# The opening of a two-block kernel: one change to the order of its loads and to the shape of two kinds of weight block

## The chip, the cores and the metric

The kernel runs on one core of a Trainium2 chip. The metric is device time in microseconds (us) of one launch. In the profile PE is TensorE (matmuls; PEld is its weight load), DVE is VectorE, ACT is ScalarE, POOL is GpSimd, and SP is SyncE, which here only issues transfers. "SPq" and "ACTq" rows are transfers issued by SP and ACT. Everything is float32.

## The reference

The program computes one Conformer-style block and then two layers of a second block on x (512 tokens x 1024). Only what the opening computes matters here:

```python
sc_l = jax.nn.silu(c)
mod_l = sc_l @ w_mod[0] + b_mod[0]                    # (1024) x (1024 x 6144)
sh1_l, s1_l, g1_l, sh2_l, s2_l, g2_l = jnp.split(mod_l, 6, axis=-1)
hl = rms_norm(xl, norm1_g) * (1 + s1_l) + sh1_l
u = hl @ w_pw1 + b_pw1                                # 1024 x 2048
a, gate = jnp.split(u, 2, axis=-1)
u = a * jax.nn.sigmoid(gate)
u = dwconv(u, w_dw) + b_dw                            # width 31, in 8 segments of 64
u = jax.nn.silu(layer_norm(u, ln_g, ln_b)) @ w_pw2 + b_pw2
xl = xl + g1_l * u
xl = xl + g2_l * (square(relu(modulate(rms_norm(xl, norm2_g), sh2_l, s2_l) @ w1)) @ w2)
```

The second block has its own modulation matrix in each layer (`ada_w_2`, 1024 x 6144 each), an attention and a convolution mixer, and a mixture of 16 experts in each layer.

## The kernel before

**Weights.** All weight matrices are streamed by SP through a ring of six slots of 2 MB (`RING`, `BLK`). The list `stream` is written out once, in order of use; entry n takes the next slot, and SP issues it when the block that held the slot has been released (`owner_release`: a semaphore and the value it must reach). A block is 1024 rows x 512 columns, loaded as 128 partitions x 8 x 512, so that each contiguous piece in memory is 2 KB (`blk`).

**Modulation.** Nine rounds (`mod_gemv`, L914 to L924) each compute 2048 modulation values from four blocks. PE multiplies the stationary silu(c) by the block's rows: 8 steps k of 128 rows, and in each 4 matmuls for the 4 groups q of 512 columns. Before, block q holds all rows of group q, and the round waits for all four blocks before its first matmul. Rounds 1 and 2 lie in the convolution stage, rounds 3 to 8 in the first multilayer perceptron, one after each fourth tile of `mlp_w1`. After a round, ACT copies the row out of PSUM (`mod_row`, L614), PE transposes it (L929), ACT copies that (`mod_turned`, L621), and POOL adds the bias and makes the gains (L473 to L502).

**Vectors.** 33 small transfers bring the vectors (c, gains, biases, convolution taps) as rows into `vec_rows`. Before, ACT issues all of them at its start (L550), and then the six transfers that make up `small_in` (four `lam` vectors and two router matrices, L577 and L579). PE turns the rows into columns in two tiles (`T_V`), DVE copies these to `vecT` (L1367, L1372), and ACT takes silu(c) from there (L632).

**The order of the opening** is the order in which each engine's code is written. SP: x, the constants `K` (1 MB in one transfer), a wait for all 33 vectors, then the ring. PE: the transposes of x (`T_X`), of the vectors (`T_V`), the mean of squares (`norm_stat(NORM1)`, L898), modulation round 0, its transposes, then the pointwise product. ACT: silu(c), the squares (L597), the root (L603), and the copies of round 0. DVE: the copies of x, those of the vectors, the `lam` sums (L1382), and then `scale(NORM1)`: a reciprocal (L1342) and eight products into hT (L1344), of which ACT shifts each (L610).

**The pointwise product** `pw1` (PE, L878) makes 16 output tiles of 128 channels, two for each j (gate, then a). Before, the gate columns of four j are one block and the a columns of the same four j another. Two pairs of blocks serve the 16 tiles. A depthwise convolution on PE (L966) stands behind each second j.

Of the kernel before, what the change touches and what calls it, by code (L numbers as in the profile page):

```python
# [12 lines left out]
P = 128  # L13
D = 1024
DT = D // P
N = 512
# [6 lines left out]
TAPS = 31  # L23
PAD = TAPS // 2
SHIFTS = 4
# [4 lines left out]
HD = 64  # L30
# [34 lines left out]
KW = _at  # L65

# [35 lines left out]
def block_kernel(nc, A, out):  # L102
# [22 lines left out]
    def add_mod(rnd):  # L125
        return [add(blk(mods[rnd // 3], 0, (rnd % 3) * 2048 + q * N), ("mod_row", rnd + 1)) for q in range(4)]
# [97 lines left out]
    for n, (src, slot) in enumerate(stream):  # L224
        if n == FIRST:
            MOE_LOADS[0] = list(loads)
            loads = [x + MOE_BLOCKS // RING for x in loads]
        loads[slot] += 1
        landed_at.append((slot, 16 * loads[slot]))
        prev_of.append(prev[slot])  # L230
        prev[slot] = n
# [8 lines left out]
    with ExitStack() as ctx:  # L240
# [49 lines left out]

        def carve(base, at, *shape):
# [59 lines left out]
        for name in (  # L351
            "vec_in", "x_in", "ctx_in", "const_in", "small_in", "stored",
# [28 lines left out]
        def arrived(eng, n):  # L381
            slot, value = landed_at[n]
            eng.wait_ge(landed[slot], value)
            return slot_ap(stream[n][1])
# [4 lines left out]
        BIASED = {NORM1: 0, LN: 1, NORM2: 2, MIX0: 3, CTXN: 4, FFN0: 5, MIX1: 6, FFN1: 7}  # L389

# [3 lines left out]
        def _(sp):  # L394
            def load(n):
# [5 lines left out]
                sp.dma_start(slot_ap(slot), src).then_inc(landed[slot], 16)  # L401
# [50 lines left out]
        def _(pool):  # L452
# [57 lines left out]
            pool.wait_ge(S["const_in"], 16)  # L510
# [31 lines left out]
        def _(act):  # L542

            g0 = [("c", 0), ("c_2", 8), ("norm2_g", 32), ("norm1_g", 24), ("conv_b_pw1", 48), ("conv_b_dw", 64),
                  ("conv_ln_g", 72), ("conv_ln_b", 80), ("conv_b_pw2", 88)]
            n_vec = 0

            def rows(dst, src):
                nonlocal n_vec
                act.dma_start(dst, src).then_inc(S["vec_in"], 16)  # L550
                n_vec += 1

            for name, at in g0:
                w = A[name].shape[1] // P
                rows(vec_rows[at:at + w, 0, :], A[name][0].rearrange("(r p) -> r p", p=P))
            for name, at in (("c_ctx_2", 16), ("final_g", 40)):
                rows(vec_rows[at:at + 8, 0, :], A[name].rearrange("(r p) -> r p", p=P))
            for name, at in (("norm_mix_2", 96), ("norm_ffn_2", 112)):
                rows(vec_rows[at:at + 16, 0, :], A[name].rearrange("l (r p) -> (l r) p", p=P))
            rows(vec_rows[0:48, 1, :], A["b_mod"][0].rearrange("(r p) -> r p", p=P))  # L560
            rows(vec_rows[48:96, 1, :], A["ada_b_2"][0].rearrange("(r p) -> r p", p=P))
            rows(vec_rows[96:120, 1, :], A["conv_w_2"][0].rearrange("k (r p) -> (k r) p", p=P))
            for m, name in enumerate(("attn_q_norm_2", "attn_k_norm_2")):
                for half in range(2):
                    rows(vec_rows[120 + m:121 + m, 1, half * HD:(half + 1) * HD], A[name])
            rows(vec_rows[122:123, 1, :], A["attn_subln_2"])
            rows(vec_rows[0:48, 2, :], A["ada_b_2"][1].rearrange("(r p) -> r p", p=P))
            for g in range(ROUNDS):
                n = min(SHIFTS, TAPS - SHIFTS * g)
                rows(vec_rows[32 * (g % 4):32 * (g % 4) + 32, 3 + g // 4, 0:32 * n].rearrange("q (k i) -> q k i", k=n),  # L570
                     A["conv_w_dw"][0][SHIFTS * g:SHIFTS * g + n].rearrange("k (q i) -> q k i", i=32))
            for m, j in enumerate(DVE_CONV):
                dst = vec_rows[0:TAPS, 5, :] if m == 2 else vec_rows[48 + TAPS * m:48 + TAPS * (m + 1), 2, :]
                rows(dst, A["conv_w_dw"][0][:, j * P:(j + 1) * P])
            assert n_vec == N_VEC
            for m, name in enumerate(("lam_q1_2", "lam_k1_2", "lam_q2_2", "lam_k2_2")):
                act.dma_start(lam_in[:, m, :], A[name][0].partition_broadcast(P)).then_inc(S["small_in"], 16)  # L577
            for layer in range(2):
                act.dma_start(rw[:, layer, :, :], A["router_w_2"][layer].rearrange("(k p) e -> p k e", p=P))\  # L579
                    .then_inc(S["small_in"], 16)  # L580

# [282 lines left out]
        def _(pe):  # L864
# [49 lines left out]
            def mod_gemv(rnd):  # L914
                ws = [arrived(pe, n) for n in B_MOD[rnd]]
# [773 lines left out]
```

## Time and profile before

| | us |
|---|---|
| median of 3 runs | 2659.02 (2658.41 to 2660.11) |
| the profiled execution's own time | 2660.16 |
| its span, first to last instruction | 2658.4 |
| PE busy, matmuls | 2385.5 (90%) |
| DVE, ACT, POOL busy | 707.2, 414.4, 60.9 |
| mean transfer rate | 213 GB/s, 565.49 MB |

The page cuts the span into 40 slices of 66 us. PE is busy for 4 tenths of the first slice and for 9 or 10 in most others; the transfers are busy for 8 tenths of it. A row of a timeline gives start and duration in us, the engine, the line and the operation, and how many instructions were merged; in brackets stands the idle time ahead of it and what ended it. A matmul of float32 appears as two records. What counts in such a kernel is what PE waits for, and where; idle time on the other engines costs nothing by itself.

### The profile page before, as it was taken

Reading aid. Unit: us, or ns where it says so; the run is one execution under the profiler, and the core shown is the slowest. Engines: PE = TensorE matmul, PEld = TensorE weight load, DVE = VectorE, ACT = ScalarE, POOL = GpSimd, SP = SyncE. Lnnn points to the kernel's source line nnn. Section 1 sums busy time; section 2 is a strip of 40 time slices with the busy share of each in tenths; the row PEclk is TensorE's granted clock in tenths of the full one; section 3 lists DMA queues with packets and bytes.
Section 4 is the critical chain, followed back from the end, with each engine's and each line's share of the span. In section 5 each row is a group of like instructions: output and inputs, shape, how many; then the busy total and the mean of one; then the engine's idle time right before and its main releaser. Section 6 shows DMA issues by size and latency. Waiting matters only on the chain.

```text
span 2658.4 us, 21610 instructions
## 1 busy us (share of the span) xinstructions
PE 2385.5 (90%) x8882; PEld 1080.2 (41%) x8882; DVE 707.2 (27%) x958; ACT 414.4 (16%) x683; POOL 60.9 (2%) x66
## 2 busy tenths in 40 slices
PE   4999899999999999677699899998999699989997
PEld 1443344444444455443334344442444334434443
DVE  2683200000006632772411111113111411111112
ACT  1223200000004111551300000001000201000000
POOL 1000000000010000000100000000000100000000
PEclk7999999999999999887899999999999899999999
DMA  8307276138300002000488999888110488999985
GB/s 293 124 35 284 96 275 230 63 133 293 143 0 32 32 32 95 0 1 0 190 354 378 391 391 380 379 379 337 42 64 0 190 346 374 388 390 390 385 379 221
DMA packets 110548, 565.49 MB, mean 213 GB/s; under 512 B 8344, under 2 KB 8734, under 8 KB 85918
## 3 DMA queue, kind: packets, MB, share of 16 engines
q1 hardware_dynamic: 105856, 563.09, 52.6%
q10 hardware_dynamic: 4638, 1.64, 0.3%
q8 instruction: 39, 0.64, 0.1%
q14 instruction: 15, 0.12, 0.0%
HBM read 562.61 MB, written 2.10 MB: 212 GB/s over the span
## 4 chain that ended last, share of the span: by engine, by line
PE 79%; DMA 9%; DVE 6%; issue 3%; ACT 2%; SPq 1%; ACTq 0%; DVEq 0%
PE psum L878 38%; PE psum L1242 19%; DMA ring<-in_moe_w_down_dram 9%; PE psum L1292 5%; PE psum L1256 5%; PE psum L1080 2%; PE psum L922 2%; PE psum L966 1%; PE psum L1149 1%; PE psum L898 1%; PE psum L1128 1%; DVE rstd L1536 1%; DVE rstd L1342 1%; PE psum L1193 1%; PE psum L1142 1%
## 5 line engine op out<-in xcount | busy, mean ns | idle before, releaser
L878 PE MATMUL psum<-hT,ring 128*128 128x512 f32 x1632 | 718.0, 600 | 23.7 <-ACT hT L610 18.4
L1242 PE MATMUL psum<-ring,arena 128*64 128x512 f32 x3072 | 681.7, 600 | 57.5 <-DMA ring<-in_moe_w_down_dram 23.7
L878 PEld LDWEIGHTS psum<-hT,ring 128*128 128x128 f32 x1632 | 312.5, 193 | 419.7 <-issue 412.9
L1242 PEld LDWEIGHTS psum<-ring,arena 128*64 128x64 f32 x3072 | 245.8, 138 | 460.6 <-issue 460.6
L878 PE MATMUL psum<-arena,ring 128*128 128x512 f32 x640 | 275.2, 592 | 0.0
L878 PEld LDWEIGHTS psum<-arena,ring 128*128 128x128 f32 x640 | 121.6, 190 | 153.1 <-issue 153.1
L1611 DVE TENSOR_TENSOR arena<-psum,arena 128x512 f32<-128x512 f32 x32 | 33.7, 1054 | 445.7 <-PE psum L1242 445.7
L1256 PE MATMUL psum<-arena 128*128 128x128 f32 x1024 | 121.9, 281 | 23.4 <-DVE arena L1602 23.4
L1256 PEld LDWEIGHTS psum<-arena 128*128 128x128 f32 x1024 | 119.0, 197 | 35.1 <-DVE hT L1622 32.1
L1292 PE MATMUL psum<-arena 128*128 128x512 f32 x256 | 123.3, 618 | 0.0
L1354 DVE SCALAR_TENSOR_TENSOR xT<-psum,modv,xT 128x512 f32<-128x512 f32 x32 | 24.0, 750 | 308.5 <-PE psum L878 308.5
L1622 DVE TENSOR_TENSOR hT<-hT,psum 128x512 f32<-128x512 f32 x128 | 88.0, 688 | 34.1 <-PE psum L1292 34.1
L1447 DVE TENSOR_TENSOR arena<-arena 128x512 f32<-128x512 f32 x32 | 22.1, 692 | 244.2 <-ACT arena L705 244.2
L922 PE MATMUL psum<-ring,cpad 128*32 128x512 f32 x576 | 66.3, 614 | 17.2 <-DMA ring<-in_w_mod_dram 17.2
L1619 DVE COPY arena<-psum 128x512 f32<-128x512 f32 x16 | 11.1, 692 | 262.7 <-PE psum L1242 262.7
L597 ACT ACTIVATE sq<-xT 128x512 f32<-128x512 f32 x56 | 35.1, 629 | 260.4 <-DVE xT L1354 228.9
L1292 PEld LDWEIGHTS psum<-arena 128*128 128x128 f32 x256 | 39.4, 188 | 83.6 <-DVE hT L1622 63.0
L1421 DVE SCALAR_TENSOR_TENSOR arena<-arena,vecT 128x512 f32<-128x512 f32 x90 | 72.3, 803 | 3.2
L1142 PE MATMUL psum<-K,arena 128*128 128x128 f32 x144 | 29.7, 355 | 48.4 <-DVE arena L1530 33.3
L705 ACT ACTIVATE arena<-psum 128x512 f32<-128x512 f32 x32 | 19.1, 597 | 311.8 <-PE psum L878 311.8
L1465 DVE RECIPROCAL rstd<-rms 128x512 f32<-128x512 f32 (+1 forms) x18 | 50.8, 2819 | 44.1 <-ACT rms L744 44.0
L898 PE MATMUL psum<-sq,K 128*128 128x512 f32 (+1 forms) x80 | 41.4, 665 | 13.1 <-ACT sq L597 12.8
(182 smaller groups left out, 1445.1 us busy)
## 6 DMA issues: line engine op xcount, KB each, us to landing
ring<-in_moe_w_gate_dram SPq DMA_DIRECT2D x64, 2048.0 KB, 16.8
ring<-in_moe_w_up_dram SPq DMA_DIRECT2D x64, 2048.0 KB, 14.2
ring<-in_moe_w_down_dram SPq DMA_DIRECT2D x64, 2048.0 KB, 14.5
ring<-in_ada_w_dram SPq DMA_DIRECT2D x24, 2048.0 KB, 10.8
ring<-in_mlp_w_dram SPq DMA_DIRECT2D x16, 2048.0 KB, 12.8
ring<-in_w_mod_dram SPq DMA_DIRECT2D x12, 2048.0 KB, 13.1
ring<-in_conv_w_pw_dram SPq DMA_DIRECT2D x6, 2048.0 KB, 18.6
ring<-in_conv_w_in_dram SPq DMA_DIRECT2D x6, 2048.0 KB, 19.0
```

What stands on the lines that cost most here:

```text
L597: act.activation(sq[:, g % 2, 0:width], src[:, j, :], ACT.Square).then_inc(S["sq_ready"], 1)
L878: ins = pe.matmul(bank[:, 0:width], w[:, k, col:col + P], src(k), start=start and k == 0, stop=stop and k == kts - 1)
L898: ins = pe.matmul(psum[:, STAT, 0:width], const("ones_d"), sq[:, g % 2, 0:width], start=j == 0, stop=j == DT - 1)
L922: ins = pe.matmul(psum[32 * q:32 * q + 32, MISC, :], cpad[:, k, :], ws[q][:, k, :], start=k == 0, stop=k == DT - 1, skip_group_check=True)
L1080: ins = pe.matmul(psum[:, t % 6, 0:width], src, w[:, k, 0:width], start=k == 0, stop=k == DT - 1)
L1142: ins = pe.transpose(psum[:, 6 + k // 4, (k % 4) * P:(k % 4 + 1) * P], attn[:, it % 2, k * P:(k + 1) * P], ident)
L1242: ins = pe.matmul(psum[64 * e:64 * e + 64, bank + nh, :], src[:, 4 * h + k, 64 * e:64 * e + 64], w[:, k, nh * N:(nh + 1) * N], start=h == ...
L1256: ins = pe.matmul(psum[:, 6 + fj // 4, (fj % 4) * P:(fj % 4 + 1) * P], h_tok[:, tt, fj * P:(fj + 1) * P], sel[:, tt, :, :].rearrange("p a ...
L1292: pe.matmul(psum[:, 6 + fj % 2, :], y_sb[:, fj * P:(fj + 1) * P], gselT, start=True, stop=True)\
L1421: ins = dve.scalar_tensor_tensor(out=acc, in0=u, scalar=w, in1=acc, op0=ALU.mult, op1=ALU.add)
L1465: link(dve.reciprocal(rstd[:, 0:w], rms[:, 0:w]))
L1622: dve.tensor_tensor(hT[:, fj, :], hT[:, fj, :], psum[:, 6 + fj % 2, :], ALU.add)\
```

## The change

SP no longer waits for the vectors. It issues x and the first 512 columns of `K` (the identity and the three averaging matrices), 15 of the 33 vector transfers (convolution taps, modulation biases, `conv_w_2`), the four blocks of modulation round 0, the first pointwise block, then the rest of `K` (1504 columns, with its own semaphore `const_rest`, for which POOL waits before it builds the taps), and goes on with the ring. ACT issues the other 18 vector transfers; the six transfers of `small_in` now come behind silu(c).

A modulation block is now 256 whole rows of the round's 2048 columns (128 x 2 x 2048, contiguous pieces of 8 KB), in all nine rounds, and PE waits for block k/2 only when step k comes to it. A pointwise block now holds the gate and the a columns of two j, 256 columns each (two transfers of 1 MB, contiguous pieces of 1 KB, one semaphore), so that four blocks serve the 16 tiles; each is released when its four tiles are done.

PE computes `norm_stat(NORM1)` ahead of the vectors' transposes, ACT does squares and root ahead of silu(c), and DVE does the reciprocal ahead of its wait for the gains, and the `lam` sums behind `scale(NORM1)`. In the other norms the wait for the gains stands behind the reciprocal too.

```diff
     def add_mod(rnd):
-        return [add(blk(mods[rnd // 3], 0, (rnd % 3) * 2048 + q * N), ("mod_row", rnd + 1)) for q in range(4)]
+        a, part = divmod(rnd, 3)
+        return [add(mods[a][256 * b:256 * b + 256, 2048 * part:2048 * part + 2048].rearrange("(k p) n -> p k n", p=P),
+                    ("mod_row", rnd + 1)) for b in range(4)]
...
-    def add_pw1(b):
-        last = T_PW1[4 * b + 3] + 2
-        B_PW1[b] = (add(blk(A["conv_w_pw1"][0], 0, D + b * N), ("tile_done", last - 1)),
-                    add(blk(A["conv_w_pw1"][0], 0, b * N), ("tile_done", last)))
-
-    add_pw1(0)
-    add_pw1(1)
+    pw1_rows = A["conv_w_pw1"][0].rearrange("(k p) n -> p k n", p=P)
+    for b in range(4):
+        B_PW1[b] = add([pw1_rows[:, :, 256 * b + D * (1 - m):256 * b + D * (1 - m) + 256] for m in range(2)],
+                       ("tile_done", T_PW1[2 * b + 1] + 2))
...
-            sp.dma_start(K[:, :], A["const_k"]).then_inc(S["const_in"], 16)
-
-            sp.wait_ge(S["vec_in"], 16 * N_VEC)
+            sp.dma_start(K[:, 0:K_FIRST], A["const_k"][:, 0:K_FIRST]).then_inc(S["const_in"], 16)
+            load_rows(sp, "late")
             for n in range(FIRST):
                 load(n)
+                if n == 4:
+                    sp.dma_start(K[:, K_FIRST:KW], A["const_k"][:, K_FIRST:KW]).then_inc(S["const_rest"], 16)
...
+            load_rows(act, "early")
...
+            act.wait_ge(S["pads_zero"], 4)
+            squares(NORM1, xT, emptied(T_X))
+            root(NORM1)
             act.wait_ge(FREE["dve"], T_V + 2)
-            act.wait_ge(S["pads_zero"], 4)
             act.activation(cpad[:, :, 0:3], vecT[:, 0:24].rearrange("p (i k) -> p k i", i=3), ACT.Silu)\
                 .then_inc(S["c_silu"], 1)
-            squares(NORM1, xT, emptied(T_X))
-            root(NORM1)
...
             def mod_gemv(rnd):
-                ws = [arrived(pe, n) for n in B_MOD[rnd]]
...
                 for k in range(DT):
+                    if k % 2 == 0:
+                        w = arrived(pe, B_MOD[rnd][k // 2])
                     for q in range(4):
-                        ins = pe.matmul(psum[32 * q:32 * q + 32, MISC, :], cpad[:, k, :], ws[q][:, k, :],
+                        ins = pe.matmul(psum[32 * q:32 * q + 32, MISC, :], cpad[:, k, :], w[:, k % 2, q * N:(q + 1) * N],
...
+            norm_stat(NORM1)
             pe.wait_ge(S["vec_in"], 16 * N_VEC)
...
-            norm_stat(NORM1)
             mod_gemv(0)
...
                 dve.wait_ge(S["rms_ready"], n + 1)
                 link(dve.reciprocal(rstd[:, 0:width], rms[:, 0:width]))
+                if made:
+                    dve.wait_ge(S["gains"], made)
...
+            scale(NORM1, xT, hT, gain[:, 0, :], made=1)
             dve.wait_ge(S["small_in"], 16 * 6)
```

SP's instructions at the start, before. `hT` receives x, `arena` the vector rows; each row is the line, the operation, the operands, the shape, what it waits for, and a count.

```order
L429 DMA hT<-in_x_dram 128x4x1024
L430 DMA K<-in_const_k_dram 128x2016
L401 DMA ring<-in_w_mod_dram 128x8x512 [waits vec_in]
L401 DMA ring<-in_w_mod_dram 128x8x512 x3
L401 DMA ring<-in_conv_w_pw_dram 128x8x512 x2
L401 DMA ring<-in_conv_w_pw_dram 128x8x512 [waits mod_row] x2
L401 DMA ring<-in_w_mod_dram 128x8x512 [waits mod_row] x2
```

The same place now:

```order
L471 DMA hT<-in_x_dram 128x4x1024
L472 DMA K<-in_const_k_dram 128x512
L400 DMA arena<-in_conv_w_dw_dram 32x4x32 x7
L400 DMA arena<-in_conv_w_dw_dram 32x3x32
L400 DMA arena<-in_conv_w_dw_dram 31x128 x3
L400 DMA arena<-in_b_mod_dram 48x128
L400 DMA arena<-in_ada_b_dram 48x128
L400 DMA arena<-in_conv_w_dram 24x128
L400 DMA arena<-in_ada_b_dram 48x128
L443 DMA ring<-in_w_mod_dram 128x2x2048 x4
L441 DMA ring<-in_conv_w_pw_dram 128x8x256 x2
L477 DMA K<-in_const_k_dram 128x1504
```

The wait for `vec_in` is gone from SP, and 15 small transfers stand where it was.

PE's instructions between the transposes of x and the pointwise product, before (`arena` holds the vector rows, `sq` the squares, `cpad` silu(c)):

```order
L888 MATMUL psum<-K,arena 128x128 [waits dve_free,vec_in]
L888 MATMUL psum<-K,arena 128x123
L898 MATMUL psum<-sq,K 128x512 [waits sq_ready] x8
L922 MATMUL psum<-ring,cpad 32x512 [waits landed3,landed2,c_silu,landed1,landed0]
L922 MATMUL psum<-ring,cpad 32x512 x31
L929 MATMUL psum<-K,mod_rows 128x128 [waits mod_row_sb]
L878 MATMUL psum<-hT,ring 128x512 [waits h_ready,landed4,dve_free]
```

The same place now:

```order
L909 MATMUL psum<-sq,K 128x512 [waits sq_ready] x8
L899 MATMUL psum<-K,arena 128x128 [waits dve_free,vec_in]
L899 MATMUL psum<-K,arena 128x123
L934 MATMUL psum<-ring,cpad 32x512 [waits landed0,c_silu]
L934 MATMUL psum<-ring,cpad 32x512 x7
L934 MATMUL psum<-ring,cpad 32x512 [waits landed1]
L934 MATMUL psum<-ring,cpad 32x512 x7
L934 MATMUL psum<-ring,cpad 32x512 [waits landed2]
L934 MATMUL psum<-ring,cpad 32x512 x7
L934 MATMUL psum<-ring,cpad 32x512 [waits landed3]
L889 MATMUL psum<-hT,ring 128x512 [waits h_ready,dve_free,landed4]
```

The statistics moved ahead of the vectors, and the one wait for four blocks became four waits of one block each.

## Rows read from the trace of the kernel before

**Rows 1.** Chain of waits, 0 to 450 us: start, us, what.

```profile
59.10 3.36 DVE rstd L1342
...
64.25 30.19 PE psum L878 x64
...
208.89 6.87 PE psum L922 x64
...
340.33 7.00 PE psum L922 x64
...
375.44 7.00 PE psum L922 x64
```

**Rows 2.** Timeline of PE, 0 to 70 us.

```profile
11.63 5.17 PE L888 MATMUL psum<-K,hT 128*128 128x128 f32 x32 [11.63 <-DMA K<-in_const_k_dram]
16.75 0.93 PE L888 MATMUL psum<-K,arena 128*128 128x128 f32 x6
20.38 9.21 PE L898 MATMUL psum<-sq,K 128*128 128x512 f32 x16 [2.70 <-ACT sq L597]
46.79 9.73 PE L922 MATMUL psum<-ring,cpad 128*32 128x512 f32 x64 [17.20 <-DMA ring<-in_w_mod_dram]
57.24 0.65 PE L929 MATMUL psum<-K,mod_rows 128*128 128x128 f32 x4 [0.71 <-ACT mod_rows L614]
```

**Rows 3.** What SP's transfers waited for, to 460 us: total, times, longest.

```profile
SPq L401 <- DMA arena<-in_conv_w_dw_dram: 15.0, 1, 15.0
```

**Rows 4.** Timeline of SP, 0 to 460 us.

```profile
1.25 0.49 SPq L430 DMA_DIRECT2D K<-in_const_k_dram  x1
16.72 15.24 SPq L401 DMA_DIRECT2D ring<-in_w_mod_dram  x4
```

**Rows 5.** Ring blocks issued at 16.72; 26.12; 215.8 and 216.2 us: issue to landing.

```profile
DMA to landing us min/median/max: 13.5/13.5/13.5
...
DMA to landing us min/median/max: 20.4/20.4/20.4
...
DMA to landing us min/median/max: 7.8/10.3/12.8
```

**Rows 6.** Transfers by issue, 0 to 60 us: count, KB each, us to landing.

```profile
hT<-in_x_dram SPq DMA_DIRECT2D x1, 2048.0 KB, 8.1
...
K<-in_const_k_dram SPq DMA_DIRECT2D x1, 1008.0 KB, 10.3
rw<-in_router_w_dram ACTq DMA_DIRECT2D x2, 64.0 KB, 11.4
```

**Rows 7.** Windows: PE, PEld, DVE, ACT, POOL busy; granted clock, DMA share, GB/s.

```profile
29.60:46.80 17.20, 0.01 (x2) 0.04 (x3) 0.46 (x4) 0.80 (x2) 0.00 (x0) 0.56 1.05 387
64.25:69.40 5.15, 5.15 (x7) 2.15 (x8) 3.97 (x8) 5.13 (x8) 0.00 (x0) 0.51 1.05 387
1630.00:1700.00 70.00, 62.51 (x303) 27.38 (x301) 10.97 (x15) 6.04 (x8) 0.00 (x0) 1.00 0.93 393
```

**Rows 8.** Timeline of ACT, 0 to 70 us.

```profile
9.16 5.06 ACTq L550 DMA_DIRECT2D arena<-in_conv_w_dw_dram  x11
...
16.09 1.10 ACTq L579 DMA_DIRECT2D rw<-in_router_w_dram  x2
...
19.58 0.23 ACT L632 ACTIVATE cpad<-vecT 128x24 f32<-128x24 f32 x1 [0.95 <-DVE vecT L1372]
...
56.59 0.60 ACT L614 ACTIVATE mod_rows<-psum 128x512 f32<-128x512 f32 x1 [26.18 <-PE psum L922]
```

**Rows 9.** Timeline of DVE, 0 to 70 us.

```profile
12.79 0.69 DVE L1363 COPY xT<-psum 128x512 f32<-128x512 f32 x1 [11.89 <-PE psum L888]
...
18.09 1.23 DVE L1367 COPY vecT<-psum 128x128 f32<-128x128 f32 x4
...
62.49 5.44 DVE L1344 SCALAR_TENSOR_TENSOR hT<-xT,gain,rstd 128x512 f32<-128x512 f32 x8
```

**Rows 10.** What PE's instructions waited for, 64.3 to 500 us: total, times, longest.

```profile
PE psum L878 <- ACT hT L610: 12.4, 2, 6.4
```

More of the change, by code:

```diff
@@ L227, in block_kernel @@
             loads = [x + MOE_BLOCKS // RING for x in loads]
-        loads[slot] += 1
+        loads[slot] += len(src) if isinstance(src, list) else 1
         landed_at.append((slot, 16 * loads[slot]))
@@ L289, in slot_ap, with slot_like @@
             return ring[:, slot * BLK:(slot + 1) * BLK].rearrange("p (k n) -> p k n", k=DT)
+        def slot_like(slot, src):
+            whole = ring[:, slot * BLK:(slot + 1) * BLK]
+            if isinstance(src, list):
+                return [carve(whole, m * BLK // 2, src[m].shape[1], src[m].shape[2]) for m in range(2)]
+            return whole.rearrange("p (k n) -> p k n", k=src.shape[1])
         def carve(base, at, *shape):
@@ L400, in load @@
                     sp.wait_ge(S[name], value)
-                sp.dma_start(slot_ap(slot), src).then_inc(landed[slot], 16)
+                if isinstance(src, list):
+                    for m, dst in enumerate(slot_like(slot, src)):
+                        sp.dma_start(dst, src[m]).then_inc(landed[slot], 16)
+                else:
+                    sp.dma_start(slot_like(slot, src), src).then_inc(landed[slot], 16)
             def load_experts(layer):
@@ L556, in _ @@
[L556 to L580, printed above, removed]
+            load_rows(act, "early")
@@ L628, in _ @@
             act.sem_inc(S["y_act"], 1)
+            act.wait_ge(S["pads_zero"], 4)
+            squares(NORM1, xT, emptied(T_X))
+            root(NORM1)
             act.wait_ge(FREE["dve"], T_V + 2)
[L631 removed]
             act.activation(cpad[:, :, 0:3], vecT[:, 0:24].rearrange("p (i k) -> p k i", i=3), ACT.Silu)\
                 .then_inc(S["c_silu"], 1)
[L634 to L635 removed]
+            for m, name in enumerate(("lam_q1_2", "lam_k1_2", "lam_q2_2", "lam_k2_2")):
+                act.dma_start(lam_in[:, m, :], A[name][0].partition_broadcast(P)).then_inc(S["small_in"], 16)
+            for layer in range(2):
+                act.dma_start(rw[:, layer, :, :], A["router_w_2"][layer].rearrange("(k p) e -> p k e", p=P))\
+                    .then_inc(S["small_in"], 16)
             mod_row(0)
@@ L1335, in link, with scale @@
                 dve.wait_ge(S["dve_link"], link_n[0])
-            def scale(n, src, dst, gains, width=N):
+            def scale(n, src, dst, gains, width=N, made=0):
                 if n:
@@ L1385, in _ @@
                 dve.wait_ge(S["lam_sum"], m + 1)
-            dve.wait_ge(S["gains"], 1)
-            scale(NORM1, xT, hT, gain[:, 0, :])
             def glu(j):
@@ L1440, in _ @@
                 dve.tensor_tensor(xT[:, j, :], xT[:, j, :], tmp[:, j % 2, :], ALU.add).then_inc(S["x_pw2"], 1)
-            dve.wait_ge(S["gains"], 3)
-            scale(NORM2, xT, hT, gain[:, 1, :])
+            scale(NORM2, xT, hT, gain[:, 1, :], made=3)
             for half in range(2):
@@ L1451, in _ @@
             scale(FINAL, xT, xT, vec("final_g"))
-            dve.wait_ge(S["gains"], 8)
-            scale(MIX0, xT, hT, gain[:, 2, :])
+            scale(MIX0, xT, hT, gain[:, 2, :], made=8)
             scale(CTXN, xcT, hcT, gain[:, 3, :], NC)
```

51 lines of the change are left out of this document (35 added, 16 removed).

## The prediction

> **What bounds the kernel now.** I read the page first: PE is busy for nine tenths of most slices and for four tenths of the first, while the transfers are busy there. The whole question is therefore when the first pointwise matmul starts. The chain of waits has it at 64.25 us, as the head of an unbroken run on PE [rows 1]. In the timeline of PE before that [rows 2] the reader is to see five short pieces and one idle stretch that dwarfs the rest: 17.20 us ahead of modulation round 0, ended by a transfer of `w_mod`. SP's waits say why it came late: SP stood 15.0 us for the vectors [rows 3] and issued the first modulation block at 16.72 [rows 4]. That block landed 13.5 us later, at 30.2, and the fourth, issued at 26.12, landed 20.4 later, at 46.5 [rows 5], where PE starts. Behind 64.25, up to 500 us, PE waits for hT twice (12.4 us in all, one of them the 6.4 us at 64.25) and for no transfer [rows 10]. So a shift of the first pointwise matmul should reach the end almost whole, and nothing but that shift is on offer.
>
> **The start.** Before, x landed at 0.75 + 8.1 = 8.85 (its issue stands 0.5 us ahead of that of `K`), and `K` at 1.25 + 10.3 = 11.55 [rows 4, 6]; PE starts at 11.63 [rows 2]. Only a quarter of `K` now stands ahead: of the 2.7 us between the two landings some 0.7 stay, so the transposes of x start at 9.6 and, at 5.1 us, end at 14.7. This is not on the path by itself (below).
>
> **SP's issues.** After x and `K` SP issues 15 small transfers. ACT took 5.06 us for 11 such [rows 8], 0.46 each, so 15 take 6.9, and the first modulation block is issued at 1.75 + 6.9 = 8.6 instead of 16.72: 8.1 us earlier. ACT's own 18, at the same 0.46, end by 9. All vectors are in by some 2.5 us after the last issue, as before (14.2 to 16.75), thus by 11 to 13.
>
> **The landing of the four blocks.** Two bounds. In a batch late in the trace, with nothing else in flight, the first block landed after 7.8 us and the second, 0.4 later issued, after 12.8, that is 5.4 us apart [rows 5]. From 8.6 that gives 16.4, 21.8, 27.2, 32.6. In the opening itself the first took 13.5, though the rate of the idle stretch is full at 387 GB/s, 5.4 us per block [rows 7]: 5.7 us went to the vectors' successors, two router matrices and four `lam` vectors in tiny pieces, which took 11.4 us to land beside the blocks [rows 6]. These are still issued, now behind silu(c) at about 27, so they meet blocks 3 and 4. Fourth block: 32.6 to 38.3. I take 35, nearer to the undisturbed batch, because the first two blocks are through before they come.
>
> The Trainium skill has a rule against this change here ("DMA: Bandwidth & Descriptors", Why a DMA increments its semaphore by 16 and not by 1): the number of DMA engines must divide the outermost size, so a transfer of 31 rows runs on one engine alone. The three 31-row transfers now stand ahead of the modulation blocks in the same queue, and every block needs all 16 engines. No row of this trace shows the engines apart. By the rule one engine would be late with all four blocks, and the fourth would land towards the later bound; without it towards the earlier.
>
> **Round 0.** The statistics (9.21 us [rows 2]; its first squares follow the first copy of x, 1.2 us behind the first transpose [rows 2, 9]) run 14.7 to 23.9, the two vector tiles 0.93, and silu(c) ends 3.1 us after their start (16.75 to 19.81 [rows 2, 8]; the root, now ahead of it on ACT, has the 2.8 us in which PE and DVE make the columns, from 18.09 before [rows 9]). Round 0 can start at 27. The statistics have moved ahead of silu, which costs 9 us on PE but inside time that PE would wait anyway; that cover is thin now, not 17 us. From 27 its 64 records took 9.73 us with a granted clock that began at the lower level, and take 6.87 at the higher [rows 1, 2], 13.7 wholly at the lower. With block 4 at 35 and only its quarter left, the end is 35 + 1.7 to 3.4, and by PE's own pace 27 + 9.7 = 36.7. I take 37.3. Before: 56.5.
>
> **From round 0 to the pointwise product.** Before, 64.25 - 56.52 = 7.7 us [rows 1, 2]. In it stands the reciprocal of 3.36 us [rows 1], whose input is there soon after the statistics (29.6 [rows 2]), but which stood behind the wait for the gains. It now runs beside the modulation round (root at about 25, done by 31). What stays is copy, transposes, copy, bias, gain, one product (the first of the eight from 62.49 [rows 9]), one shift: 4.4 us. The first pointwise matmul could start at 41.7. What becomes late next is its weight block: it lands one block behind the fourth, 35 + 5.4 = 40.4 if 1 KB pieces move as fast as 2 KB ones, and 35 + 10.8 = 45.8 if a piece of 1 KB costs as much time as one of 2 KB, which halves the rate. The lower bound is 5.4, for a shorter piece gives no reason to move faster. x (4 KB pieces), the blocks (2 KB) and the experts (16 KB) move at 8.1 us a block with its latency, 387 and 393 GB/s [rows 6, 7], so the cost of a piece is small beside its bytes at 2 KB; I take 6 us, thus 41.
>
> The Trainium skill puts the smallest piece for line rate at 512 B ("DMA: Bandwidth & Descriptors", Specifications). By it the block lands at 40.4 and PE never waits for it. No run so far shows 1 KB pieces.
>
> I take **42.0** for the first pointwise matmul. It begins at the lower clock, as before (0.51 from 64.25 to 69.40 [rows 7], where half clock costs 2.6 us); I count no difference, and plus or minus 2.6 for the range.
>
> **Edits at nothing.** The rest of `K` (0.77 MB, 2 us) lands near 43 to 45; POOL needs it for the taps, 1.9 us each, which the first convolution reads 30 us after the first pointwise matmul (64 records [rows 1]): cover 20 us. The second block lands at about 50 and is needed at 72. The `lam` sums (0.5 us on DVE) now stand ahead of the first gating; all of `small_in` is issued by 30 and, by its 11.4 us, in at 42; the gating starts behind the first two tiles, 15 us after the pointwise start, at 57. If the router pieces were slowed threefold the cover would be gone and DVE, which is nearly full in the convolution stage, would run late with it. ACT issues six transfers (1.10 us for the last two [rows 8]) between silu(c) and the copy of the round's row, at 27 to 30, against 37. The blocks of later rounds are requested at the same points or earlier, since pointwise blocks are released after 4 tiles, not 8, and no round up to 500 us but the first waited for one [rows 10]. The reciprocal of later norms gains nothing: there the gains are long made.
>
> **Sum.** Fourth block 46.5 - 35 = 11.5 us (8.1 from the earlier issue, 3.4 of the 5.7 that the tiny pieces cost); end of the round behind that block 10.0 - 2.3 = 7.7; reciprocal 3.4; less the 0.3 by which I place the start behind 41.7. Together 22.3, from 64.25 to 42.0. Against the profiled execution, 2660.16 (its span of 2658.4 and 1.8 around it): 2637.9. The median of the runs is 1.1 lower, and I predict 0.6 of that off: **2637.3**.
>
> **Rivals.**
> A. *The transfers are later than I have them*: small pieces and the single-engine rows push block 4 to 38.3, or the 1 KB pieces cost as much as those of 2 KB. Then the pointwise start is at 38.3 + 10.8 = 49 at worst, in one of the two cases 45 or 46. Gain 15 to 19: 2641 to 2644. For it: 13.5 against 7.8 us [rows 5]. Against: the tiny pieces now come behind two of the blocks.
> B. *Whole rows of 8 KB move slowly* (the side of slower). All nine rounds load this way. In the perceptron a round, with its block of `mlp_w1`, must load 5 blocks in the 35.1 us between two rounds (340.33 to 375.44 [rows 1]): it binds above (35.1 - 5.4)/4 = 7.4 us per block, and over six such rounds it eats the 22 us from 8.3 us per block (6 x 4 x 0.9), which is 253 GB/s. At half rate (10.8 us) each round is 13.5 late: 81 us more in the perceptron, no gain in the opening, 2740. Against it: pieces of 16 KB run at 393 GB/s [rows 7], and x in pieces of 4 KB landed 8.1 us after its issue, as a ring block alone does.
> C. *The shift is taken back later*, by a stage that transfers bind. The expert stage is near that: 393 GB/s, share 0.93 [rows 7]. But its loads wait for the slots that the attention frees, so they start earlier too. If it held, no change: 2659.
>
> **Chances and range.** My forecast 0.82, as a range of its own 2633 to 2641; A 0.12; B 0.03; C 0.03. The range holds the forecast's and A's: from 2632.5 (pointwise start at 39.5 and the 2.6 us of low clock gained, less what both rarely give together) to 2644.5. No change is told apart at about 0.2%, 5 us. Faster 0.94, same 0.03, slower 0.03.
>
> **What would show it.** The first `w_mod` issue on SP at 8 to 9.5. PE: statistics from about 15, round 0 from 27 in up to four pieces with waits for the ring, its end at 36 to 39. DVE's reciprocal ahead of that end. The first pointwise matmul at 40 to 44, released by hT and not by the ring (by the ring: rival A). The taps, the `lam` sums and the gating waiting for no transfer. From the first pointwise matmul to the end of the span 2594 us, as before, within 3. Wrong would be: a wait for `w_mod` or `ada_w` in rounds 1 to 8 (B), more waits for `moe_w_down` (C), or ACT's copy of the round's row later than PE's last matmul, held by its own issues.

## The result, and the profile after

Four runs of the changed kernel gave a median of 2639.48 us (2635.09 to 2640.19), against 2659.14 us for the kernel before: a ratio of 0.9922, with a 95% interval of 0.9905 to 0.9940, or 19.7 us. The forecast was 2637.3, and the range of 2632.5 to 2644.5 holds the time.

Timeline of PE after, start and duration in us, with the idle time ahead and what ended it:

```profile
10.35 6.06 PE L899 MATMUL psum<-K,hT 128*128 128x128 f32 x32 [10.35 <-DMA K<-in_const_k_dram]
16.25 7.60 PE L909 MATMUL psum<-sq,K 128*128 128x512 f32 x16
23.69 0.87 PE L899 MATMUL psum<-K,arena 128*128 128x128 f32 x6
26.27 5.36 PE L934 MATMUL psum<-ring,cpad 128*32 128x512 f32 x48 [1.71 <-ACT cpad L640]
34.72 2.75 PE L934 MATMUL psum<-ring,cpad 128*32 128x512 f32 x16 [3.09 <-DMA ring<-in_w_mod_dram]
38.16 1.12 PE L941 MATMUL psum<-K,mod_rows 128*128 128x128 f32 x4 [0.70 <-ACT mod_rows L620]
44.05 26.48 PE L889 MATMUL psum<-hT,ring 128*128 128x512 f32 x55 [4.78 <-ACT hT L616]
```

The 17.20 us of [rows 2] have shrunk to 3.09. Round 0 is worked off as its blocks land: the first three quarters run without a pause, and only the fourth waits for its block. The first pointwise matmul is at 44.05 instead of 64.25: 20.2 us. Here are SP's issues, where the 15.0 us of [rows 3] are gone, and DVE and ACT where they answer to [rows 8, 9]:

```profile
1.79 7.18 SPq L400 DMA_DIRECT2D arena<-in_conv_w_dw_dram  x11
...
10.65 2.13 SPq L443 DMA_DIRECT2D ring<-in_w_mod_dram  x4
12.83 17.16 SPq L441 DMA_DIRECT2D ring<-in_conv_w_pw_dram  x2
```

```profile
26.13 3.35 DVE L1353 RECIPROCAL rstd<-rms 128x512 f32<-128x512 f32 x1
40.52 5.39 DVE L1357 SCALAR_TENSOR_TENSOR hT<-xT,gain,rstd 128x512 f32<-128x512 f32 x8 [11.04 <-POOL gain L545]
```

```profile
27.67 4.94 ACTq L645 DMA_DIRECT2D rw<-in_router_w_dram  x2
37.51 0.60 ACT L620 ACTIVATE mod_rows<-psum 128x512 f32<-128x512 f32 x1 [11.29 <-PE psum L934]
41.37 5.30 ACT L616 ACTIVATE hT<-hT,modv 128x512 f32<-128x512 f32 x8 [1.87 <-DVE hT L1357]
```

The reciprocal is off the path. SP stood from 13.36 to 30.0 in the issue of the second half of the first pointwise block (most of the 17.16), so the rest of `K` went out only at 30.03. The windows show the rates: pieces of 8 KB at 427 GB/s (first), a hole while the six transfers of `small_in` were in flight, in pieces of 256 and 64 B (second), pieces of 1 KB at 347 (third). Columns as in [rows 7].

```profile
20.00:26.00 6.00, 4.56 (x15) 1.88 (x14) 1.55 (x8) 5.16 (x7) 0.00 (x0) 1.00 1.01 427
30.00:36.00 6.00, 2.91 (x28) 0.68 (x24) 0.00 (x0) 0.00 (x0) 0.00 (x0) 0.97 0.80 262
46.00:60.00 14.00, 14.00 (x30) 6.03 (x29) 3.23 (x6) 2.64 (x4) 3.78 (x2) 0.88 1.10 347
```

Issue to landing of the first and the fourth modulation block (issued at 10.65 and 12.14) and of the second half of the first pointwise block (13.36):

```profile
DMA to landing us min/median/max: 8.2/8.2/8.2
...
DMA to landing us min/median/max: 22.5/22.5/22.5
...
DMA to landing us min/median/max: 30.7/30.7/30.7
```

They landed at 18.9, 34.7 and 44.0. The last is the moment at which PE starts, while ACT's first shift of hT ends near 42.1. The profile names hT as the releaser; the landing says that it was the block, and a second profile of the same kernel names it:

```profile
44.25 30.20 PE L889 MATMUL psum<-hT,ring 128*128 128x512 f32 x64 [4.92 <-DMA ring<-in_conv_w_pw_dram]
```

A second landmark, far behind the opening, is the context projection in the attention (96 records of 128x256), here before and after:

```profile
L878 PE MATMUL psum<-ring x96: 379/379/631, 888.5 to 955.5; 128*128 128x256 f32 x96
```

```profile
L889 PE MATMUL psum<-ring x96: 379/379/634, 868.2 to 935.2; 128*128 128x256 f32 x96
```

It starts 20.3 us earlier, and the last instruction 20.0 (2638.4 against 2658.4). The shift of the opening reached the end whole. Behind the landmark lie 1770.2 us after and 1769.9 before.

### The profile page after: what moved, and what is told of

Read it like the earlier page. It is cut to its first block, busy times and chain, and to the rows that moved or that the text cites. A ratio compares the mean times of both kernels' runs of the same rounds, so it can differ in the third digit from the quotient of the medians.

```text
span 2638.4 us, 21617 instructions
## 1 busy us (share of the span) xinstructions
PE 2378.7 (90%) x8882; PEld 1079.2 (41%) x8882; DVE 710.3 (27%) x958; ACT 416.5 (16%) x684; POOL 61.1 (2%) x66
## 4 chain that ended last, share of the span: by engine, by line
PE 77%; DMA 12%; DVE 6%; ACT 2%; issue 2%; SPq 1%; DVEq 0%; POOL 0%; ACTq 0%; POOLq 0%
PE psum L889 38%; PE psum L1253 17%; DMA ring<-in_moe_w_down_dram 11%; PE psum L1267 5%; PE psum L1303 5%; PE psum L1091 2%; PE psum L934 2%; PE psum L977 1%; PE psum L1160 1%; PE psum L909 1%; PE psum L1139 1%; DMA ring<-in_w_mod_dram 1%; DVE rstd L1546 1%; PE psum L1204 1%; DVE rstd L1353 1%
## 5 line engine op out<-in xcount | busy, mean ns | idle before, releaser
L1253 PE MATMUL psum<-ring,arena 128*64 128x512 f32 x3072 | 676.7, 596 | 63.8 <-DMA ring<-in_moe_w_down_dram 32.1
L1267 PEld LDWEIGHTS psum<-arena 128*128 128x128 f32 x1024 | 119.4, 197 | 35.1 <-DVE hT L1632 32.1
L1139 PE MATMUL psum<-ring 64*128 64x256 f32 (+1 forms) x192 | 46.7, 615 | 3.5 <-ACT arena L783 2.7
```

Of the source, the lines that this page charges most:

```text
L1139: ins = pe.matmul(psum[:, banks + bank, at:at + hi - lo], qT[64 * c:64 * c + 64, h, m * P:(m + 1) * P], kT[64 * c:64 * c + 64, h, lo:hi], ...
L1253: ins = pe.matmul(psum[64 * e:64 * e + 64, bank + nh, :], src[:, 4 * h + k, 64 * e:64 * e + 64], w[:, k, nh * N:(nh + 1) * N], start=h == ...
L1267: ins = pe.matmul(psum[:, 6 + fj // 4, (fj % 4) * P:(fj % 4 + 1) * P], h_tok[:, tt, fj * P:(fj + 1) * P], sel[:, tt, :, :].rearrange("p a ...
```

## The experiments

All are edits of the changed kernel. "Start" is the first pointwise matmul, "landmark" the start of those 96 records; both come from each run's profile. Times of single runs say little: the same kernel's stretch behind the landmark moved by 3.3 us between two profiles of the change, and by 6.8 between two of the old order. "Both", the two kernels with two blocks first and "taps last" all contain the edit "small_in late", so their start is to be compared with its 40.48.

| | start | landmark | span |
|---|---|---|---|
| before | 64.25 | 888.5 | 2658.4 |
| the change | 44.05 | 868.2 | 2638.4 |
| SP waits again | 47.07 | 868.8 | 2639.1 |
| modulation in columns | 53.18 | 878.1 | 2648.4 |
| pointwise blocks in pairs | 42.63 | 866.8 | 2636.8 |
| engines' old order | 45.61 | 867.8 | 2634.5 |
| small_in late | 40.48 | 864.9 | 2635.3 |
| 31-row transfers on ACT | 43.40 | 865.4 | 2636.0 |
| both | 43.34 | 868.0 | 2638.0 |
| two blocks first | 40.80 | 865.5 | 2632.7 |
| the same, taps behind | 42.58 | 867.1 | 2637.2 |
| the change again | 44.25 | 868.1 | 2635.0 |
| old order again | 45.85 | 870.3 | 2643.8 |
| taps last | 37.44 | 859.4 | 2629.4 |

**SP waits again.**

```diff
             load_rows(sp, "late")
+            sp.wait_ge(S["vec_in"], 16 * N_VEC)
```

> The changed kernel, but SP again waits for all 33 vector transfers before the first ring block; everything else stays. If the early issue past that wait is what pays (theory A, 8 us of the 20), the first pointwise matmul goes from 44.05 us to about 52. If it is the order and place of the small transfers that pays and the wait itself is nearly empty by then (theory B: the last small one is issued at 10.3 us and lands some 2.5 later, so SP would stand only about 2.5 us), it goes to about 46.5 and the time to about 2642.

One run, 2640.94 us. The first block was issued at 13.96 instead of 10.65, and the start came 3.0 us later. Theory B holds: with the small transfers at the front of SP's own order the wait costs 3.0 us, not 8. The landmark is only 0.6 later, because the higher clock was granted for longer here, in two places: from the start on, and in the statistics of the second norm (16 records near 210 us). These are the windows after this edit and in the change:

```profile
47.07:52.07 5.00, 5.00 (x9) 2.26 (x10) 5.00 (x6) 3.41 (x6) 3.39 (x2) 0.71 1.09 351
211.29:218.89 7.60, 7.60 (x16) 2.43 (x16) 3.40 (x6) 5.33 (x8) 0.00 (x0) 1.00 1.05 387
```

```profile
44.05:49.05 5.00, 5.00 (x6) 2.19 (x7) 3.90 (x6) 3.90 (x5) 2.99 (x2) 0.50 1.09 349
209.10:218.20 9.10, 9.10 (x16) 3.06 (x16) 3.40 (x6) 5.33 (x8) 0.00 (x0) 0.81 1.04 384
```

Nine records against six in the first 5 us; the first 64 pointwise records took 29.52 us against 30.34, which is 0.8, and the statistics another 1.5. Together they are nearly all of the 2.4 us by which the landmark is closer to the start. What decided the granted level in either place is not shown.

**Modulation in columns**, with PE waiting for all four blocks again.

```diff
-        return [add(mods[a][256 * b:256 * b + 256, 2048 * part:2048 * part + 2048].rearrange("(k p) n -> p k n", p=P),
-                    ("mod_row", rnd + 1)) for b in range(4)]
+        return [add(blk(mods[rnd // 3], 0, (rnd % 3) * 2048 + q * N), ("mod_row", rnd + 1)) for q in range(4)]
```

> The changed kernel, but modulation blocks are column blocks as before (1024 rows x 512 columns, pieces of 2 KB), and a round waits for all four. If the rows pay by letting round 0 be worked off as they land (theory A), round 0 starts only when the fourth block is in, at 35 to 37 us, takes 7 to 13 us, and the first pointwise matmul is at 48 to 53: 4 to 9 us lost. If the rows pay only through the size of their pieces (theory B: 425 instead of 387 GB/s), 2 us are lost, 46.

One run, 2650.2 us; the start is 9.1 us later, the landmark 9.9. PE:

```profile
38.26 9.05 PE L931 MATMUL psum<-ring,cpad 128*32 128x512 f32 x64 [13.93 <-DMA ring<-in_w_mod_dram]
```

The fourth block lands at 38.0 instead of 34.7, and the round, 9.05 us, stands wholly behind it, where only 2.75 did: 6.3 us are overlap. Of the 3.3 us of landing, the rate in the quiet stretch explains some 2.1 (an estimate: pieces of 2 KB had 386 GB/s from 20 to 26 us, where those of 8 KB had 427, which is 5.4 against 4.9 us a block). Most of the rest is in the last block, 7.6 us behind the third against 5.9 in the change; `small_in` was in flight beside it in both.

The end of the round is 9.8 us later, the start 9.1. Of the round's delay 1.8 was hidden, because the change waited that long for the pointwise block anyway; but here POOL's first tap (49.77, just behind the gains) ran beside the first product, and ACT had it 1.5 us later than in the change, where its shift at 41.37 waited 1.87:

```profile
52.31 0.72 ACT L614 ACTIVATE hT<-hT,modv 128x512 f32<-128x512 f32 x1 [3.42 <-DVE hT L1354]
```

Among the parts that an experiment took back, the row blocks are the largest.

**Pointwise blocks in pairs** of 2 KB pieces, as before.

```diff
-    for b in range(4):
-        B_PW1[b] = add([pw1_rows[:, :, 256 * b + D * (1 - m):256 * b + D * (1 - m) + 256] for m in range(2)],
-                       ("tile_done", T_PW1[2 * b + 1] + 2))
+    add_pw1(0)
+    add_pw1(1)
```

> The changed kernel, but the pointwise blocks are as before (gate and a blocks of 512 columns, four j, pieces of 2 KB). Theory A: the first pointwise matmul at 44.05 us waited for the second half of its block (pieces of 1 KB, landed at 44.1) and not for hT, though the profile names hT: with 2 KB pieces and one block to wait for it starts when hT is there, at 42.2, and the time falls by 2 us. Theory B: the profile's name is right and the hT chain set 44.05: no change. Against both, if the small-piece transfers of ACT cost it and not the 1 KB pieces: about 42 to 43.

One run, 2638.63 us. Start at 42.63: 1.4 us earlier, with a wait that now names the block.

```profile
42.63 30.35 PE L892 MATMUL psum<-hT,ring 128*128 128x512 f32 x64 [3.22 <-DMA ring<-in_conv_w_pw_dram]
```

PE needs only this one block, the gate columns, for its first tile; it landed at 42.5, where hT was ready near 42.4. The block set the start of the change, not hT, as theory A has it. The new shape of the pointwise block costs a little in this kernel.

**The engines' old order** in the opening, with the new loads (PE part of the edit; ACT and DVE likewise).

```diff
-            norm_stat(NORM1)
             pe.wait_ge(S["vec_in"], 16 * N_VEC)
...
+            norm_stat(NORM1)
             mod_gemv(0)
```

> The changed kernel with the order on PE, ACT and DVE as before (vectors transposed and silu(c) made ahead of the statistics; the reciprocal behind the wait for the gains), loads unchanged (the six small_in transfers now behind the root on ACT). Theory A: the reciprocal alone pays, 3.4 us, of which the 1.9 us that the pointwise block is late anyway hide a part: first pointwise matmul 46 to 47. Theory B: the statistics now in front of round 0 also delay it (start 29 instead of 26), and 47.5 to 49 results. If the reordering of the engines pays nothing, 44.

> The changed kernel itself again, beside the next run, on one chip. First pointwise matmul at 44.05, and the span behind it 2594 us within 3. It says what part of the differences of 1 to 4 us between the single runs belongs to the rest of the program.

> The kernel with the engines' old order of the opening and the new loads, again. Its one run had the first pointwise matmul 1.6 us later (45.6) but a time 3 us lower (2636.3) than the change. Theory A: the lower time came from the expert stage, which varies from run to run; timed in rounds it is 0 to 2 us slower than the change. Theory B: the old order is really faster by some 3 us, and it will show in both the median and the profile.

Start at 45.61 and, again, 45.85, against 44.05 and 44.25: the new order gains 1.6 us. The reciprocal takes its 3.35 on the path again (40.75, behind the gains), of which the late pointwise block hides half. Round 0 starts at 26.9 against 26.3. The low time of the first run (2636.29) came from elsewhere: in rounds on one chip the old order had 2638.56 (0.9925, 0.9911 to 0.9938), the change 2636.83 (0.9920, 0.9906 to 0.9933), which the intervals do not separate. The stretch behind the landmark was 1770.2 and 1766.9 in two runs of the change, 1766.7 and 1773.5 in two of the old order.

**small_in late**, issued by ACT in the perceptron stage.

```diff
-            for m, name in enumerate(("lam_q1_2", "lam_k1_2", "lam_q2_2", "lam_k2_2")):
-                act.dma_start(lam_in[:, m, :], A[name][0].partition_broadcast(P)).then_inc(S["small_in"], 16)
...
             shift(NORM2, hT, modv[:, 0, 24:32])
+            for m, name in enumerate(("lam_q1_2", "lam_k1_2", "lam_q2_2", "lam_k2_2")):
+                act.dma_start(lam_in[:, m, :], A[name][0].partition_broadcast(P)).then_inc(S["small_in"], 16)
```

> The changed kernel, but the six small_in transfers (four lam vectors in pieces of 256 B, two router matrices in pieces of 64 B) are issued by ACT in the perceptron stage and the lam sums are made before the norm FINAL; nothing of them is in flight in the opening. Theory A (tiny pieces hold up the ring blocks: they cost the fourth modulation block some 1.2 us and the pointwise block some 3): fourth block at 33.5, pointwise block at 39.5, first pointwise matmul set by hT at 41: 3 us gained, 2636. Theory B (the pieces of 1 KB themselves make the block late): pointwise block still 9 us behind the fourth modulation block, 43 to 44, no gain.

Median 2636.86 us (0.9928, 0.9911 to 0.9944). Start at 40.48, landmark 3.3 us earlier than in the change. The fourth block landed at 34.2, only 0.5 earlier, but the pointwise block at 40.0 instead of 44.0: 5.9 us behind the fourth, which is 2 MB at 357 GB/s, where the change had 9.3. Here hT sets the start (40.48) by a little. The hole is gone:

```profile
30.00:36.00 6.00, 3.17 (x32) 0.60 (x24) 0.00 (x0) 0.00 (x0) 0.00 (x0) 1.00 1.04 368
```

So the six transfers cost 3.5 us on the pointwise block, and the 1 KB pieces some 0.5 beside the 5.4 us of a block in 2 KB pieces. The two router matrices (64 B) and the four `lam` vectors (256 B) were moved together, so which of them made the hole is not shown. The total in rounds does not show these 3 us.

**31-row transfers on ACT**, and **both**.

```diff
+                for m, j in enumerate(DVE_CONV):
+                    dst = vec_rows[0:TAPS, 5, :] if m == 2 else vec_rows[48 + TAPS * m:48 + TAPS * (m + 1), 2, :]
+                    rows(dst, A["conv_w_dw"][0][:, j * P:(j + 1) * P])
             else:
```

> The changed kernel, but the three 31-row transfers are issued by ACT behind its 18, not by SP. Theory A (what counts is SP's issue time: the 11 tap transfers took 7.2 us, these three the last 2 to 3 of them): the first modulation block is issued at 8.3 instead of 10.65, and everything up to the first pointwise matmul is 2 us earlier, 42. Theory B (a single slow engine holds the modulation blocks because 31 rows go through one): also the gap between the blocks' landings at the end shrinks from 5.3 to 4.5 us. Rival C: the vectors now arrive beside 8 KB pieces and are slowed; silu(c) comes later than 26 us and eats the gain.

> The small_in transfers late (as in the run before the last) and the three 31-row transfers on ACT, together. If the two gains add: fourth modulation block at 31.5, round 0 over at 34.5, first pointwise matmul at 39, against 44.05: 5 us, 2634. If the first pointwise matmul is set by something else than transfers, it stays above 41.

2637.79 (one run) and 2636.11 us (0.9925, 0.9902 to 0.9948). With the first edit alone modulation was issued at 8.05, 2.6 us earlier, and its fourth block landed at 35.6, a microsecond later. The first half of rival C came true:

```profile
25.39 0.93 PE L899 MATMUL psum<-K,arena 128*128 128x128 f32 x6 [1.37 <-DMA arena<-in_conv_w_dw_dram]
```

The last of the vector rows, some now in the other queue beside 8 KB pieces, landed at 25.4 (in "SP waits again" all were in when SP's wait ended at 13.96), and silu(c) came 1.6 us late. But this did not eat the gain, as rival C has it, for PE still waited for the fourth block:

```profile
35.65 2.98 PE L934 MATMUL psum<-ring,cpad 128*32 128x512 f32 x16 [2.43 <-DMA ring<-in_w_mod_dram]
```

The blocks themselves were late: the first landed 11.9 us after its issue instead of 8.2. When it was issued, x and `K` had not landed (8.9 and 10.0), and from 9.5 to 12.5 us the transfers were busy but moved little:

```profile
9.50:12.50 3.00, 2.47 (x12) 2.47 (x13) 1.15 (x2) 0.54 (x1) 0.00 (x0) 1.00 1.09 237
```

The step from the third landing to the fourth, 5.3 us, is not the 4.5 of theory B (the change had 5.9); a single slow engine is neither shown nor excluded. The two edits do not add: together the start is at 43.34, no better than with the 31-row edit alone and 2.9 us worse than with `small_in` late alone.

**Two blocks first**, and **the same, taps behind**.

```diff
-            load_rows(sp, "late")
             for n in range(FIRST):
+                if n == 2:
+                    load_rows(sp, "late")
                 load(n)
...
             pool.wait_ge(S["const_rest"], 16)
+            pool.wait_ge(S["scaled"], DT)
```

The last line is in the second of the two alone.

> The kernel with the late small_in transfers, and SP now issues the first two modulation blocks ahead of its 15 vector transfers, the other two behind them. In the runs so far nothing moved between the landing of K near 9.5 and the first modulation data near 12.5. Theory A (SP's issue time leaves the transfers idle there, and this is what bounds the opening): blocks land at 15, 20, 26 and 31 instead of 34.2, the vectors at about 21 still ahead of their use at 23.5, and the first pointwise matmul comes at 37.5 against 40.5: 3 us. Theory B (the small transfers, one of them per engine and piece, cost the same wherever they stand): no change, 40.5. Rival C: the vectors land behind 24 us and delay silu(c); then round 0 starts late, and the gain is under 1 us.

> As the run before, and POOL builds the taps only when DVE has finished the eight products of the first norm. With the reciprocal ahead of the gains, the taps (1.9 us each on POOL) ran beside these products in several runs, and the eight took 8.7 us instead of 5.4, two of them slowed by 1.6 us each, while PE read hT. Theory A (POOL and DVE hold each other up): the eight products take 5.4 again, and PE's first 64 records, which can outrun hT once its clock is up, save under 1 us. Theory B (the slow products come from the clock or the transfers): still 8.7.

2636.15 us (0.9919, 0.9905 to 0.9932) and 2635.48 (0.9910, 0.9896 to 0.9923). The first gained nothing over `small_in` late (40.80 against 40.48), as theory B says, but not for its reason. The two blocks landed early, at 14.5 and 19.6. Behind them SP was held in its own issues:

```profile
1.79 1.06 SPq L443 DMA_DIRECT2D ring<-in_w_mod_dram  x2
2.89 16.22 SPq L400 DMA_DIRECT2D arena<-in_conv_w_dw_dram  x11
...
20.79 0.95 SPq L443 DMA_DIRECT2D ring<-in_w_mod_dram  x2
```

```profile
19.00:23.00 4.00, 3.35 (x8) 0.89 (x6) 0.00 (x0) 3.33 (x5) 0.00 (x0) 1.00 0.51 110
```

Eleven issues took 16.22 us instead of 7.18, and the thin stretch of the transfers came from 19 to 23 us (half busy, 110 GB/s) instead of from 9.5 to 12.5 (in `small_in` late 0.47 and 89 GB/s). The fourth block landed at 34.5, where it had been 34.2. In the second kernel the eight products of the norm took 5.39 us again, against 8.69 in the first, where POOL's taps (2.31 and 2.35 us instead of 1.91) ran beside them:

```profile
39.09 8.69 DVE L1358 SCALAR_TENSOR_TENSOR hT<-xT,gain,rstd 128x512 f32<-128x512 f32 x8 [9.71 <-POOL gain L546]
```

```profile
40.87 5.39 DVE L1359 SCALAR_TENSOR_TENSOR hT<-xT,gain,rstd 128x512 f32<-128x512 f32 x8 [11.47 <-POOL gain L546]
```

Theory A on POOL and DVE holds, and the other profiles agree: 8.70 with both taps beside the products (`small_in` late), 7.04 where only a part fell together (pairs), 5.39 in the change, whose taps began at 46.06, behind the products. The start of the second kernel is later only because the last quarter of round 0 ran at the lower clock (3.62 us against 1.92).

**Taps last**, on top of `small_in` late. The core of the edit; the taps have their own semaphore and tile.

```diff
-    T_V = tiles(["dve"] * 2)
+    T_V = tiles(["dve"])
...
                 if n == 4:
+                    load_rows(sp, "taps")
                     sp.dma_start(K[:, K_FIRST:KW], A["const_k"][:, K_FIRST:KW]).then_inc(S["const_rest"], 16)
...
                 pw1(2 * m)
+                if m == 0:
+                    pe.wait_ge(S["tap_in"], 16 * 11)
+                    pe.wait_ge(S["tap_pad"], 1)
+                    turn_tile(T_TAP, [(vec_rows[0:VEC_ROWS[g], g, :], VEC_ROWS[g]) for g in (2, 3, 4, 5)])
```

> The kernel with the late small_in transfers, in which the convolution taps (11 of SP's 15 small transfers, 7 us of its issue time) have their own semaphore and their own transposed tile, go out on SP behind the first pointwise block, and are turned on PE and copied on DVE behind the first two pointwise tiles. Only four small transfers stand ahead of the modulation blocks. Theory A (the idle transfers between 9.5 and 12.5 us and the issue time bound the fourth block, which landed at 34.2 to 34.6 wherever the taps stood ahead of it): blocks issued from 3.5 us, landed at 14.5, 19.5, 24.5 and 29.5, round 0 from 25.7 to 32, first pointwise matmul at 36.5 to 37.5 against 40.5; the transposes cost 0.6 us on the path later, so 2.5 to 3.5 us net, 2633 to 2634. Theory B (with the blocks earlier, the order statistics, vectors, silu(c) becomes the bound): round 0 still starts at 25.7 and is worked off at PE's own pace, its end at 33 to 36, and the gain is 1 to 2 us. Rival C: the taps land too late and PE stands behind the first two tiles: the first pointwise matmul is early, but PE shows a wait for the taps.

Median 2631.20 us (2629.93 to 2632.51), ratio 0.9902, 0.9886 to 0.9919: all four runs are below the fastest of the change (2634.24), though the intervals of the two ratios overlap.

```profile
25.15 7.13 PE L938 MATMUL psum<-ring,cpad 128*32 128x512 f32 x64 [2.20 <-ACT cpad L644]
33.01 0.66 PE L945 MATMUL psum<-K,mod_rows 128*128 128x128 f32 x4 [0.72 <-ACT mod_rows L624]
37.44 15.44 PE L893 MATMUL psum<-hT,ring 128*128 128x512 f32 x32 [3.77 <-DMA ring<-in_conv_w_pw_dram]
52.71 0.65 PE L903 MATMUL psum<-K,arena 110*128 110x110 f32 x4
```

The fourth block landed at 30.3, just as PE came to its quarter; round 0 ran at the higher clock with no pause that the timeline shows and ended at 32.3, and the start is bound by the pointwise block (37.4). Theory A's numbers came out (landing 29.5, start 36.5 to 37.5), with 3.0 us gained over `small_in` late. Of theory B this much holds: the round was worked off at PE's own pace, so earlier modulation blocks alone would give nothing more while silu(c) lets it start at 25.15. PE does not wait for the taps. The landmark is 8.8 us ahead of the change's, more than the start (6.6): the clock rose early (windows), and the statistics of the second norm took 7.60 us instead of 9.10 again.

```profile
32.30:37.44 5.14, 0.66 (x5) 0.42 (x5) 2.53 (x4) 2.47 (x5) 0.66 (x3) 0.95 0.97 242
37.44:42.44 5.00, 5.00 (x9) 2.26 (x10) 2.86 (x5) 4.90 (x7) 0.00 (x0) 0.71 0.99 337
```

**What the experiments leave open.** Taken back one at a time, SP's wait, the column blocks and the old order cost 3.0, 9.1 and 1.6 us at the start, and the old pointwise pairs gained 1.4. That is 12.3 of the 20.2 us, if single edits add up at all, which the two edits above did not. The rest of the change (15 vector transfers moved to SP, `small_in` behind silu(c), the cut of `K`) no run took back.

## Why the prediction was right

- **The bound and its reach.** Right: only the start moves, by 20.2 us, and 20.3 and 20.0 are found at the landmark and the end. (From the start to the end of the span it was 2594.4 us, and 2590.8 in the second profile, just outside my 3 us around 2594.) Rival C is out. More waits for `moe_w_down`, which I had named as its sign, did appear (32.1 against 23.7 us), but 20.2 in the change's second profile, with the same landmark: this wait varies by itself.
- **The start of x**: 10.35 and 10.02 against 9.6, and the transposes took 6.06 us, not 5.1. That the vector tiles still began at 23.7, as in my sum, is luck: the 9.21 us that I took over for the statistics had been measured at a granted clock of 0.81, and at 1.00 they took 7.60.
- **SP's issues** were mis-sized: 0.46 us each came from ACT, where nothing large stood in the queue. On SP, behind x and `K`, the 11 tap transfers took 7.18, and 1.89 of it was the last alone, in SP's timeline `7.08 1.89 SPq L400 DMA_DIRECT2D arena<-in_conv_w_dw_dram  x1`. First block issued at 10.65, not 8.6.
- **The fourth block**: 34.7 against 35. That it came so close is luck, for errors cancelled. The issue was 2.0 late; but 8 KB pieces move at 427 GB/s, not 387, and the tiny pieces took 0.5 us from this block, not 2.4. Their price was right in kind and put on the wrong block: the pointwise one paid 3.5.
- **Round 0**: start 26.27 against 27, end 37.5 against 37.3. Columns show what the overlap is worth: 6.3 us, against 7.7 in the sum.
- **The chain behind it**: hT was ready for 42.2, which is 4.8 us, not 4.4; the transposes took 1.12 at the lower clock instead of 0.65.
- **The pointwise block** is the step that failed. I put it at 41 and off the path; it landed at 44.0 and set the start, 1.8 us behind hT. The 1 KB pieces (347 GB/s, so 6.0 us a block) were sized rightly; that `small_in` would be in flight beside this block too was left out of its term. By my own sign (started by the ring, not by hT) this is rival A's mechanism, 2.05 us late instead of 3 to 7. The forecast of the time is 2.2 us under the median; but the second set of runs had its median at 2636.83, half a microsecond under the forecast, so the closeness of the time says less than that of the start.
- **Rival B** is wrong in sign: whole rows of 8 KB are the faster pieces. No later round waited for its blocks.
- **The two rules of the Trainium skill** ("DMA: Bandwidth & Descriptors"). That three 31-row transfers run on one engine each and would delay the blocks (Why a DMA increments its semaphore by 16 and not by 1) made no visible step here: the first block behind them landed 8.2 us after its issue, against 7.8 to 8.2 for a block by itself. The test is weak, though: they were issued from 6.4 us on, and their 48 KB at a sixteenth of 427 GB/s would be 1.8 us (an estimate), so they may have been through by 10.65. By the rule on 512 B for line rate (Specifications) 1 KB pieces should be as fast as longer ones; they ran at 347 to 360 GB/s, 2 KB at 386, 8 KB at 427. The measurement decides.
- **Edits at nothing**: right for the path, wrong for the sign. I had the taps and the `lam` sums wait for no transfer; POOL's taps waited 5.65 us for the rest of `K` (to 46.06) and DVE's `lam` sums 1.06 for the router (to 46.98, where I had 42), both far ahead of their use. ACT's router issues took 4.94 us instead of 1.10, still ahead of the round's end.

## What to carry to other kernels

Where an opening waits for weights, cut the blocks so that each can be used as it lands, and count every issue in front of them on the queue's own engine; then look at which block is next, and at what small pieces share the transfers with it. A small transfer behind large ones in the same queue can hold the issuing engine (16.22 us for eleven here), so what is not needed yet goes last, not in the middle. When the profile names one releaser and several were waited for, compare their landing times before believing it.

## What the runs showed of the hardware

- Rate by piece size, with the transfers' share of the window at 1.01 to 1.10: 347 to 360 GB/s at 1 KB, 386 at 2 KB, 427 at 8 KB.
- Pieces of 64 and 256 B in a second queue opened a hole: DMA share 0.80 and 262 GB/s for 6 us, though large blocks stood in the first queue. Without them 1.04 and 368.
- An issue can hold the engine that makes it: SP's 11 tap transfers took 7.18 us with x and `K` ahead (1.89 of it the last one), 16.22 with two blocks of 8 KB pieces as well, and the second half of a pointwise block, behind four modulation blocks and its own first half, 16.63.
- POOL and DVE slow each other, here with operands in SBUF on both: eight products 5.4 us alone, 8.7 beside two POOL products, which grew from 1.91 to 2.3.
- The same 16 statistics records took 9.10 us at a mean granted clock of 0.81 and 7.60 at 1.00, in runs of kernels that differ only in the opening.
